# Heads of all blocks in one sequence in the prompt's sparse attention; small constants first and key and value pages in pairs in the sample's

## The reference, cut to what matters

```python
def dsa_prompt(q, k, v, iq, ik, iw):            # per block of 128 queries
    t = i * DSA_QBLOCK + jnp.arange(DSA_QBLOCK)
    sc = indexer_scores(iqb, iwb, ik)           # sum over 8 heads of relu(iq . ik) * iw
    sc = jnp.where((key_pos[None, :] <= t[:, None])[None], sc, -jnp.inf)
    _, idx = lax.top_k(sc, kk)                  # kk = 256
    return dsa_attend(qb, ks, vs, idx <= t[None, :, None])      # 8 heads, 2 key/value heads, head dim 64

def dsa_sample(...):                            # 8 samples x 8 queries, 2048 past keys in 16 pages of 128
    ks = jnp.where(in_past, cache_k[layer, phys, off], k_new[bidx, inew])   # phys = page_table[...]
    vs = jnp.where(in_past, cache_v[layer, phys, off], v_new[bidx, inew])
    return dsa_attend(q, ks, vs, idx <= t[None, :, None])
```

## Time and profile before

| | us |
|---|---|
| median of 3 runs | 3746.54 (3743.01 to 3746.85) |
| the profiled execution's own time | 3748.45 |
| its span | 3746.8 |
| sample's stage, first instruction to the next stage's first transfer | 604 to 867.6 |
| prompt's stage, heads of block 0 to the last y | 898 to 1432.6 |
| TensorE busy over the span | 3308.3 (88%) |
| VectorE busy | 1605.0 (43%) |
| mean granted TensorE clock | 0.905 of 2.4 GHz |

### The profile page before, as it was taken

How to read it: one execution, slowest core, us unless ns; L and a number is a source line. 1 busy time by engine, 2 the same in 40 slices (tenths; PEclk the granted TensorE clock), 3 DMA queues, 4 the chain that set the end, 5 groups by cost and what they waited for, 6 DMA issues and landing times. The chain is left out here.

```text
span 3746.8 us, 53513 instructions
## 1 busy us (share of the span) xinstructions
PE 3308.3 (88%) x20539; PEld 2829.9 (76%) x20539; DVE 1605.0 (43%) x2853; ACT 1089.8 (29%) x2145; POOL 340.2 (9%) x440
## 2 busy tenths in 40 slices
PE   8998884665798997999999997987997999999997
PEld 7797763343444555999999997983665999999997
DVE  2186661993676523111113564432454111113566
ACT  2223541323333233111113443212443111112443
POOL 1100102122111000000000002340000000000002
PEclk9998885786688778999999998996998999999999
DMA  4211014223000001111112111222001111112111
GB/s 130 57 35 30 24 35 118 68 67 127 29 17 17 14 15 40 45 45 45 45 39 98 39 49 48 49 69 86 32 25 43 45 45 41 43 45 94 40 56 49
DMA packets 238053, 190.85 MB, mean 51 GB/s; under 512 B 53762, under 2 KB 215956, under 8 KB 237844
## 3 DMA queue, kind: packets, MB, share of 16 engines
q1 hardware_dynamic: 230148, 170.73, 15.1%
q0 software_dynamic: 7728, 17.71, 1.5%
HBM read 158.73 MB, written 31.38 MB: 51 GB/s over the span
## 5 line engine op out<-in xcount | busy, mean ns | idle before, releaser
L1980 PE MATMUL ffn1u_ps<-h_hi,ffn1u_whi 128*128 128x384 f32 (+1 forms) x1056 | 348.0, 330 | 9.5 <-DVE h_lo L2042 9.5
L1980 PE MATMUL ffn0u_ps<-h_hi,ffn0u_whi 128*128 128x384 f32 (+1 forms) x1056 | 344.8, 327 | 8.8 <-DVE h_lo L2042 8.8
L1980 PE MATMUL ffn1u_ps<-h_lo,ffn1u_whi 128*128 128x384 f32 (+1 forms) x1056 | 347.9, 329 | 0.0
L1980 PE MATMUL ffn1u_ps<-h_hi,ffn1u_wlo 128*128 128x384 f32 (+1 forms) x1056 | 347.8, 329 | 0.0
L1980 PE MATMUL ffn0u_ps<-h_hi,ffn0u_wlo 128*128 128x384 f32 (+1 forms) x1056 | 344.9, 327 | 0.0
L1980 PE MATMUL ffn0u_ps<-h_lo,ffn0u_whi 128*128 128x384 f32 (+1 forms) x1056 | 344.8, 326 | 0.0
L197 PE MATMUL ine_ps<-ine_w_hi,ine_x_hi 128*128 128x256 f32 (+2 forms) x864 | 265.4, 307 | 5.1 <-DVE ine_w_lo L213 5.0
L197 PE MATMUL ine_ps<-ine_w_hi,ine_x_lo 128*128 128x256 f32 (+2 forms) x864 | 250.6, 290 | 0.0
L197 PE MATMUL ine_ps<-ine_w_lo,ine_x_hi 128*128 128x256 f32 (+2 forms) x864 | 250.2, 290 | 0.0
L1980 PEld LDWEIGHTS ffn1u_ps<-h_hi,ffn1u_whi 128*128 128x128 f32 x1056 | 198.9, 188 | 9.9 <-DVE ffn1u_wlo L2024 9.9
L1980 PEld LDWEIGHTS ffn0u_ps<-h_hi,ffn0u_whi 128*128 128x128 f32 x1056 | 198.7, 188 | 9.2 <-DVE ffn0u_wlo L2024 9.2
(11 more groups left out here) (464 smaller groups left out, 7344.7 us busy)
## 6 DMA issues: line engine op xcount, KB each, us to landing
ffn0u_raw<-in_ffn_w_gu_dram SPq DMA_DIRECT2D x44, 512.0 KB, 3.8
ffn1u_raw<-in_ffn_w_gu_dram SPq DMA_DIRECT2D x44, 512.0 KB, 3.8
ffn0d_w<-in_ffn_w_down_dram SPq DMA_DIRECT2D x88, 128.0 KB, 2.2
ffn1d_w<-in_ffn_w_down_dram SPq DMA_DIRECT2D x88, 128.0 KB, 2.2
smp_Kp<-in_cache_k_dram SPq DMA_DIRECT2D x128, 64.0 KB, 1.9
smp_Vp<-in_cache_v_dram POOLq DMA_DIRECT2D x96, 64.0 KB, 2.2
ine_w<-in_w_in_even_dram SPq DMA_DIRECT2D x5, 1024.0 KB
scratch_h<-ine_stage SPq DMA_DIRECT2D x20, 256.0 KB, 2.5
```

Source lines behind the costliest of these rows:

```text
L1980: last = nc.tensor.matmul(ps[:, t, k2, 0:n], wp[:, k2, k, :], hp[:, k, t0:t0 + n], start=(k == 0 and j == 0), stop=(k == KD - 1 and j == 2))
```

## The change

It has three parts.

1. **SP's order in the sample's stage.** The two transfers of `spread` and that of the samples' bias go ahead of the first page.
2. **Pages in pairs.** `load_pages` takes a list of places, and for each page read from the table issues the key page and the value page. SP loads samples 0, 2, 4, 6 and POOL samples 1, 3, 5, 7. `Vp` grows from four to eight samples, so no value page waits for a slot; the semaphores `v_last_in` go.
3. **The prompt's heads in one sequence.** Scores, row maximum and exponential of (i + 1, head 0) are issued in the turn of (i, head 7). The transposes of y(i), their copies and `scale` (from i = 1 on) move into block i + 1 behind head 0's values. `q` and `iq` stand first in a block's list; the two `out` halves are added to the shares of heads 1 and 2.

```diff
-def load_pages(eng, pages, n_pool, b, j0, j1, cache, dst_of, landed, group=4):
+def load_pages(eng, pages, n_pool, b, j0, j1, places, group=4):
...
         for r in range(group):
-            src = cache[bass.ds(at[r], 1)]
...
+            for cache, dst_of, landed in places:
+                src = cache[bass.ds(at[r], 1)]
...
+                eng.dma_start(dst_of(bass.ds(g * group + r, 1)), src).then_inc(landed, 16)
...
-        out = [("out", s, 0), ("out", s, 1)]
+        out, more = [("out", s, 0), ("out", s, 1)], []
...
-            out += [("iq", s + S0)] + dots(BLOCK[s + S0], range(4))
-        if s + 1 < NT:
-            out.append(("q", s + 1))
-        return out
+            more = [("iq", s + S0)] + dots(BLOCK[s + S0], range(4))
+        q = [("q", s + 1)] if s + 1 < NT else []
+        return q + more, out
...
-        return [(u[n * per:(n + 1) * per], r[n * rper:(n + 1) * rper]) for n in range(NH)]
+        return [(u[n * per:(n + 1) * per] + out[n - 1:n][:n], r[n * rper:(n + 1) * rper]) for n in range(NH)]
...
             slots += [("p", i, n, c) for c in range(ptg(i))]
+            if n == 0 and i >= 1:
+                slots += [("y", i - 1, 0), ("y", i - 1, 1)]
...
+                scores(0, 0)
                 for i in range(NT):
-                    scores(i, 0)
                     for n in range(NH):
                         if n + 1 < NH:
                             scores(i, n + 1)
+                        elif i + 1 < NT:
+                            scores(i + 1, 0)
                         transpose_probs(i, n)
...
                         values(i, n)
-                    pe.wait_ge(y_done, i + 1)
...
+                        if n == 0 and i >= 1:
+                            y_transposes(i - 1)
...
                         if n + 1 < NH:
                             exps(i, n + 1)
+                        elif i + 1 < NT:
+                            exps(i + 1, 0)
+                        if n == 0 and i >= 1:
+                            if i >= 2:
+                                scale(i - 1)
+                            copy_y(i - 1)
                     deviation(i)
...
                         if n + 1 < NH:
                             row_max(i, n + 1)
+                        elif i + 1 < NT:
+                            row_max(i + 1, 0)
...
-        Vp, Vn = sb("Vp", [P, 4, PAGES, P]), sb("Vn", [DEC_SEQ, NB, P])
+        Vp, Vn = sb("Vp", [P, NB, PAGES, P]), sb("Vn", [DEC_SEQ, NB, P])
...
+        def load(eng, b):
+            if b >= 4:
+                eng.wait_ge(kt_done, 4 * (b - 3))
+            key_of = lambda j: Kp[:, b % 4, j, :].rearrange("p o c -> p (o c)")
+            value_of = lambda j: Vp[:, b, j, :].rearrange("p o c -> p (o c)")
+            load_pages(eng, pages, n_pool, b, 0, PAGES, [(A["cache_k"][0], key_of, k_in[b % 4]), (A["cache_v"][0], value_of, v_in[b])])
...
-                sp.wait_ge(pin, 16)
-                load(sp, 0, A["cache_k"][0], Kp, 0, k_in[0])
-                load(sp, 1, A["cache_k"][0], Kp, 1, k_in[1])
                 for f in range(2):
                     sp.dma_start(spf[NS * f:NS * f + NS, :, :], C["spread"]).then_inc(cin, 16)
                 sp.dma_start(bias[:, :], st.bias_dram).then_inc(bias_in, 16)
+                sp.wait_ge(pin, 16)
+                load(sp, 0)
                 for b in range(NB):
                     sp.dma_start(Vn[:, b, :], Hs[8 * b:8 * b + 8, C_DV:C_DV + P]).then_inc(vn_in, 16)
...
+                for b in (2, 4, 6):
+                    load(sp, b)
...
                 pool.wait_ge(pin, 16)
-                for b in range(4):
-                    load(pool, b, A["cache_v"][0], Vp, b % 4, v_in[b % 4])
+                for b in (1, 3, 5, 7):
+                    load(pool, b)
...
-                        vs = (2 * p + b2) % 4
-                        if p < NP_ - 1:
-                            pe.wait_ge(v_in[vs], 16 * PAGES * (p // 2 + 1))
-                        else:
-                            pe.wait_ge(v_last_in[b2], 16 * PAGES)
+                        vs = 2 * p + b2
+                        pe.wait_ge(v_in[vs], 16 * PAGES)
```

More of the change, by code:

```diff
@@ L1032, in passes @@
             return [("index_keys", 0), ("index_keys", 1), ("iq", S0), ("keys", 0), ("keys", 1), ("q", 0)] + dots(BLOCK[S0], range(4))
-        out = [("out", s, 0), ("out", s, 1)]
+        out, more = [("out", s, 0), ("out", s, 1)], []
         if s == 0:
-            out += [("iq", S0 + 1)] + dots(BLOCK[S0 + 1], range(2))
+            more = [("iq", S0 + 1)] + dots(BLOCK[S0 + 1], range(2))
         elif s == 1:
-            out += dots(BLOCK[S0 + 1], range(2, 4))
+            more = dots(BLOCK[S0 + 1], range(2, 4))
         elif s + S0 < NT:
-            out += [("iq", s + S0)] + dots(BLOCK[s + S0], range(4))
-        if s + 1 < NT:
-            out.append(("q", s + 1))
-        return out
+            more = [("iq", s + S0)] + dots(BLOCK[s + S0], range(4))
+        q = [("q", s + 1)] if s + 1 < NT else []
+        return q + more, out
     def rounds(s):
@@ L1053, in shares @@
     def shares(s):
-        u, r = passes(s), rounds(s)
+        (u, out), r = passes(s), rounds(s)
         per, rper = 2 * -(-len(u) // (2 * NH)) if len(u) > NH else 1, -(-len(r) // NH)
-        return [(u[n * per:(n + 1) * per], r[n * rper:(n + 1) * rper]) for n in range(NH)]
+        return [(u[n * per:(n + 1) * per] + out[n - 1:n][:n], r[n * rper:(n + 1) * rper]) for n in range(NH)]
     pass_no, dot_no, dot_bank, dots_before = {}, {}, {}, {}
@@ L1303, in _, with y_transposes @@
                         bank7(u)
+                def y_transposes(i):
+                    T = tile(i)
+                    pe.wait_ge(y_done, i + 1)
+                    for hf in range(2):
+                        slot_free(("y", i, hf))
+                        for k in range(4):
+                            c0 = (T_GR, T_DQ)[hf] + k * P
+                            last = nc.tensor.transpose(bank(("y", i, hf))[:, k * P:(k + 1) * P], T[:, c0:c0 + P], st.ident[:, :])
+                        last.then_inc(t_done, 1)
+                scores(0, 0)
                 for i in range(NT):
-                    T, share = tile(i), shares(i)
-                    scores(i, 0)
+                    share = shares(i)
                     for n in range(NH):
@@ L1323, in _ @@
                         values(i, n)
-                    pe.wait_ge(y_done, i + 1)
-                    for hf in range(2):
-                        slot_free(("y", i, hf))
-                        for k in range(4):
-                            c0 = (T_GR, T_DQ)[hf] + k * P
-                            last = nc.tensor.transpose(bank(("y", i, hf))[:, k * P:(k + 1) * P], T[:, c0:c0 + P], st.ident[:, :])
-                        last.then_inc(t_done, 1)
+                        if n == 0 and i >= 1:
+                            y_transposes(i - 1)
+                y_transposes(NT - 1)
                 bank7(("out", NT, 0))
@@ L1403, in _, with copy_y @@
                     bank7(u)
+                def copy_y(i):
+                    for hf in range(2):
+                        act.wait_ge(t_done, number[("y", i, hf)] + 1)
+                        if hf == 0 and i >= 2:
+                            act.wait_ge(p7_done, pass_no[("out", i - 1, 1)] + 1)
+                        nc.scalar.copy(YT[:, i % 2, 4 * hf:4 * hf + 4, :],
+                                       bank(("y", i, hf)).rearrange("p (a t) -> p a t", a=4)).then_inc(t_read, 1)
+                exps(0, 0)
                 for i in range(NT):
                     share = shares(i)
-                    exps(i, 0)
                     for n in range(NH):
@@ L1414, in _ @@
                             exps(i, n + 1)
-                    deviation(i)
-                    for hf in range(2):
-                        act.wait_ge(t_done, number[("y", i, hf)] + 1)
-                        if hf == 0 and i >= 2:
-                            act.wait_ge(p7_done, pass_no[("out", i - 1, 1)] + 1)
-                        nc.scalar.copy(YT[:, i % 2, 4 * hf:4 * hf + 4, :],
-                                       bank(("y", i, hf)).rearrange("p (a t) -> p a t", a=4)).then_inc(t_read, 1)
-                    scale(i)
+                        elif i + 1 < NT:
[4 more added lines that the diff above has]
+                            copy_y(i - 1)
+                    deviation(i)
+                    if i == 0:
+                        scale(0)
+                copy_y(NT - 1)
+                scale(NT - 1)
                 copy_x(NT - 1)
@@ L1593, in dsa_sample @@
         cin, pin = sem("const_in"), sem("page_table_in")
-        k_in, v_in = [sem(f"k_pages{k}") for k in range(4)], [sem(f"v_pages{k}") for k in range(4)]
-        v_last_in = [sem("v_last_pages0"), sem("v_last_pages1")]
+        k_in, v_in = [sem(f"k_pages{k}") for k in range(4)], [sem(f"v_pages{b}") for b in range(NB)]
         bias_in, vn_in = sem("bias_in"), sem("v_new_in")
@@ L1658, in _ @@
```

(2 more changed lines are left out.)

28 lines of the change are left out of this document (10 added, 18 removed).

## The result

The changed kernel takes 3655.28 us in the median of four runs (3654.66 to 3658.62), beside 3744.78 for the kernel before (3742.02 to 3746.85): a ratio of 0.9763, 95% interval 0.9746 to 0.978, 89.5 us. The profiled executions differ by 93.6 us (3748.45 and 3654.86). The forecast was 3681, a gain of 65.4.

What follows compares the result with a forecast made beforehand. VectorE, started late by `spread`, bounds the sample's stage; in the prompt's no engine is full and two waits alternate. Gains 37.4 + (20 + 11 - 3 = 28) = 65.4 us give a median of 3681, 8-in-10 range 3654 to 3706.

Steps and rivals of the forecast that it cites:

- Part 1 and 2: Sample's stage: VectorE's chain starts earlier with `spread` ahead of the pages, paired pages give none back; 37.4 us gained.
- Part 2 costs nothing: Sample's stage: pages in pairs delay TensorE's keys, but VectorE's search rounds hide it; 0 us, without them 10 us once.
- My row for POOL's issues beside VectorE's search: Sample's stage: a MATCH_REPLACE8 of 1.21 us at 672.08 showed no slowdown from POOL's transfers; the sum holds zero.
- First term of part 3: Prompt's block boundaries: the new order crosses seven of TensorE's eight waits for y; 20 of 21 us gained.
- Second term: Prompt's stage: a quarter of the time lost at 1.2 GHz after waits comes back; 11 us, bounds 0 and 45.
- the 45 us: Prompt's stage: low-clock loss in two heads' scores and an `out` half, 6.4 us at each of seven boundaries.
- Third term: Prompt's stage: `out` in two turns gives VectorE two more turns of rounds; 0 us, at most 8 in blocks 2 and 3.
- Cost of ScalarE's chain: Prompt's stage: `scale` and y's copies ahead of head 1's probabilities' copies, and `iq`'s copy wait, cost 3 us, between 0 and 10.
- rival B: Prompt's stage: wait for y only moves and the clock falls as before; part 3 gives 6 us, 3703; chance 0.18.
- rival C: Prompt's stage: clock stays up without stalls, VectorE gains from two turns; part 3 gives 58 us, 3651; chance 0.13.
- The sum: Whole kernel: 37.4 + 28 = 65.4 us gained, giving a median of 3681 us.

Runs made afterwards that it cites:

- e2: Kernel before, with only `spread` and the samples' bias issued ahead of the first page, pages not in pairs: 3734.15 us, ratio 0.9981.
- e4: Changed kernel, but both `out` halves stand in head 1's turn: 3707.61 us, ratio 0.9903.
- e5: Changed kernel, but ScalarE runs `scale` behind the copies of y instead of ahead of them: 3664.29 us, ratio 0.978.
- e9: Changed kernel, but the dots of blocks 0 to 3, with their fillers, stand in heads 3 to 6 instead of 0 to 4: 3659.66 us, ratio 0.9759.
- e10: Changed kernel, but the `out` halves stand in heads 2 and 6 instead of 1 and 2: 3664.96 us, ratio 0.9786.
- e3: Kernel before plus the changed sample part and the new list order (`q`, `iq` first, `out` in heads 1 and 2), without overlapping heads: 3724.82 us, ratio 0.9944.
- e11: Changed kernel, but both `out` halves in head 1, and three filler products ahead of the values of heads 5 to 7, blocks 0 to 6: 3675.77 us.
- e1: Kernel before, with only the sample's stage changed (constants first, pages in pairs): 3709.3 us, ratio 0.9909.
- e6: Changed kernel without the filler products ahead of every second dot (`hold_clock` calls out): 3664.84 us, ratio 0.9804.
- e8: Changed kernel, with three more filler products ahead of the values of heads 5, 6 and 7 in blocks 0 to 6: 3650.15 us, ratio 0.9749.

## Why the prediction was right, and where it was not

**Part 1 and 2, 37.4 us forecast, 36.0 measured.** The sample's stage began 2.75 us earlier after, so its rows are to be read with 2.75 added. The first weighting came at 614.39 + 2.75 = 617.1 instead of 616.3: VectorE waited 1.12 us for the second relu where I had allowed 0.4 for the lost stock. Its end moved from 851.04 to 815.1, the forecast was near 815. A pair of pages cost SP 1.87 us (a group of four every 7.5 us) against 1.85 from the earlier trace rows, and a sample cost POOL 32 us against my 31 to 34. The keys of pair 1 landed at 675.5 (forecast 676) and TensorE's wait was 7.23 us, under the 8 to 12 that I had named, as TensorE arrived later. VectorE never waited for it. "Part 2 costs nothing" holds, but it undersells the part: by e2 it carries 27 of the 36 us, which I hadn't worked out. My row for POOL's issues beside VectorE's search said nothing, as it fell between two groups of them. The answer is in the sums: 62 MATCH_REPLACE8 rows took 70.8 us both before and after, with 96 and then 128 page transfers from POOL beside them. No contention between the two shows.

**First term of part 3, 20 us forecast, 22.9 measured.** The seven waits are gone entirely, also those of small blocks; the eighth is 0.92 us. I took seven eighths of all eight, but the eighth was only 1.0 of the 23.9 us. VectorE's wait for `out` fell only from 125.2 to 116.7, so this is not where the stage was shortened.

**Second term, the clock: 11 us forecast, 34.7 measured. This is the step that failed.** I reasoned that the slow instructions begin ahead of the boundary, in heads without dots, and that most of the 45 us would stay. They do still begin there (2.07 us at 1196.59), but the low stretches recorded around the boundaries behind blocks 1 to 6 shrank from 147 us to 102. Of these 44 us, 41 lie around the boundaries behind blocks 4 and 5: there a stretch began 24 and 22 us ahead of y and now begins 10 and 9 ahead, and it ended 14 and 13 us behind it and now ends 4 and 9 behind. My 45 us were also too small a whole: they counted two heads' scores and a half of `out`, while the stage had 226.3 us of low time, worth 113. And blocks 2 to 4 all have 32 rounds (block 4 has VectorE busy for 51.77 of 71.99 us), where I wrote that few or none are left from block 4 on. From the first scores to the last y the blocks took 480 us instead of 535; I had forecast 506. The price rule cited from the Trainium skill ("TensorE: Matmul & The Clock Gate", section "HAM oscillation — how this bites in real kernels"), low time at half of itself, fits better than my differences of single rows: in five kernels with the same products and almost no waits for y (after, e4, e5, e9, e10) the stage less half its low time is 420.9 to 429.7 us, while its length goes from 492.9 to 554.4. By it the clock and the waits give 57.6 us where 55.6 came. It is a good price, not an exact one, as e3 shows with 11.2 us beside it.

**Third term, `out` in two turns: 0 forecast, and the overlap would be worth 2.2 us without it.** I had asked only what the turns do for VectorE's rounds. They decide over 52.7 us, most of it through the clock (e4, and e11 for the cause), while the same order without the overlap loses 11.8 (e3). The two edits can't be priced apart. It also shows that my bounds for the clock, 0 and 45, lay on one side only (against e1, the low time rose by 46 us in e3 and by 30 in e4): rival B's 6 us is nearly what e4 shows, and rival C's 58 is nearly what the change itself gave.

**Cost of ScalarE's chain, 3 us forecast.** New waits for copies of y are 3.4 us and those for probabilities grew by 4.1 and 2.0; small waits for `out`'s bank (3.5) and relu (2.1) went. The rest, 423.2 against 444.2 - 22.9 = 421.3, leaves a cost of 1.9 us, within the error of the half. With `scale` out of the way the profiled stage was longer, not shorter (e5).

**The sum.** 37.4 + 28 = 65.4 against 36.0 + 55.6 = 91.6 in the stages; 3655.28 us is 1.3 us inside the low end of the range, near rival C's 3651, to which I gave 0.13. The parts of the sample's stage and the waits for y came out as worked out; that the total still fell within the range was luck, since the clock term was a third of what it turned out to be and the third term had its cause wrong.

**What stays open.** Why the low time takes just these values. Filling the standstill lowers it, it is higher where an instruction of 1.14 us was moved (one execution, e5), and unchanged blocks move with changed ones (e9, e10); no run here gives a rule that would have told 157 us from 186 or 255 in advance. How much of a stage's low time varies between executions of one kernel is known only for before's order, which was profiled three times.

## What to carry to other kernels

In a stage whose TensorE is busy but in small products, read the time at the low clock beside the waits and price it at about half of itself; a reorder can move it either way by more than the wait that it removes, so its term needs a range on both sides. A long run of dense work in one place (both `out` halves in one head) can be worse than the same work in two. When a blocked constant is moved to the front of a queue, look at once at what the engine wants next: here the keys of each pair, which had to come over two queues to keep the gain.

## What the runs showed of the hardware

- The same prompt's stage, with the same instructions on every engine and at most 3.0 us of standstill for y, took 492.9 to 554.4 us, and half the low time accounts for all but 8.8 us of the difference (e9, after, e10, e5, e4).
- One program's executions can lie 48.8 us apart with their mean granted clock at 0.916 and 0.902 (e6), while the changed kernel's repeat within 4 us.
- 63 filler products of 512 columns cost 11.8 us and bought 19.0 (e8); in the order of e4 they cost 26 and bought 71 (e11). What they bought is half the fall of the low time, what they cost is the rest of the change in length.
- A pair of 64 KB pages took 1.87 us of SP's time, table read included, and 2.0 us of POOL's (a group of four pairs every 8.0 us) while both ran; neither slowed the other much beyond the 1.85 and 1.95 worked out from the rows of before.
- MAX8 and MATCH_REPLACE8 of 1024 columns took 1.21 to 1.23 us each before and after, whether POOL issued 96 or 128 page transfers beside them.
